# Hybrid decoder layer on one core: four heads of the samples' state products behind each piece of the gates' stage instead of sixteen behind each fourth

## What is computed

```python
# S_t = e^{g_t} S_{t-1} + beta_t k_t (v_t - e^{g_t} S_{t-1}^T k_t)^T ;  o_t = S_t^T q_t / sqrt(dk)
u_new = u_c - jnp.einsum('bhcd,bhde->bhce', w_c, S)
o = (jnp.einsum('bhcd,bhde->bhce', q_c * jnp.exp(G_c)[..., None], S)
     + jnp.einsum('bhcs,bhse->bhce', qk_c, u_new))
```

## Time and profile before

| | before |
|---|---|
| median of 3 runs | 2876.35 us (2874.61 to 2878.93) |
| the profiled execution's own time | 2873.98 us |
| its span, first to last instruction | 2872.4 us |
| mean granted TensorE clock | 0.957 |
| PE busy (matmul) | 2694.1 us, 94% of the span |
| DVE busy | 1658.9 us, 58% |
| ACT busy | 1344.4 us, 47% |
| POOL busy | 429.7 us, 15% |
| DMA | 505.31 MB, mean 176 GB/s |

### The profile page before, as it was taken

One profiled execution on the slowest core, in us unless ns is written; L12 is line 12 of the kernel. 1 busy time (PEld: TensorE's weight loads), 2 busy tenths in 40 slices (PEclk: granted clock), 3 DMA queues, 4 the chain that ended last, 5 costly groups with the idle time before them and its releaser, 6 DMA issues.

```text
span 2872.4 us, 57080 instructions
## 1 busy us (share of the span) xinstructions
PE 2694.1 (94%) x21133; PEld 2651.4 (92%) x21133; DVE 1658.9 (58%) x2851; ACT 1344.4 (47%) x2024; POOL 429.7 (15%) x813
## 2 busy tenths in 40 slices
PE   6989898888888989999999999899999999999997
PEld 4989898888888889999999999899999999999987
DVE  4747474747474656553335555555666656776664
ACT  4535353534344445443334434344555545665553
POOL 1324151515151505000000000000011000100000
PEclk9999999999999999999999999999999999999999
DMA  5545353535353535666665555755898566986552
GB/s 168 166 119 156 113 157 109 161 104 159 103 159 110 154 109 155 173 188 191 183 195 158 174 179 168 232 170 160 261 312 289 181 197 206 318 286 194 164 164 91
DMA packets 449338, 505.31 MB, mean 176 GB/s; under 512 B 27713, under 2 KB 429882, under 8 KB 446338
## 3 DMA queue, kind: packets, MB, share of 16 engines
q1 hardware_dynamic: 415264, 415.42, 48.1%
q0 software_dynamic: 24640, 86.42, 9.3%
q10 hardware_dynamic: 9282, 1.24, 0.3%
HBM read 477.10 MB, written 26.49 MB: 175 GB/s over the span
## 4 chain that ended last, share of the span: by engine, by line
PE 76%; POOL 8%; DMA 4%; issue 4%; DVE 3%; ACT 3%; POOLq 0%; ACTq 0%; DVEq 0%; SPq 0%
PE bank L668 75%; POOL prod L539 4%; POOL sol L542 4%; ACT whi L941 1%; DMA blk<-blk_scratch 1%; DMA raw<-in_w_ffn_down 1%; DMA raw<-in_w_o 1%; DMA sol_scratch<-sol 1%; DMA DT<-sol_scratch 1%; DVE wlo L1233 0%; ACT xhi L955 0%; DVE E L1285 0%; POOLq L73 0%; POOL sol_scratch L564 0%; POOL DT L568 0%
## 5 line engine op out<-in xcount | busy, mean ns | idle before, releaser
L668 PE MATMUL bank<-xhi,whi 128*128 128x264 f32 x5520 | 1618.9, 293 | 34.4 <-DVE wlo L1233 17.0
L668 PE MATMUL bank<-xlo,whi 128*128 128x264 f32 x5520 | 1593.3, 289 | 0.0
L668 PE MATMUL bank<-xhi,wlo 128*128 128x264 f32 x5520 | 1590.3, 288 | 0.0
L1233 DVE TENSOR_TENSOR wlo<-raw,whi 128x1024 fp32r<-128x1024 f32 x828 | 1012.1, 1230 | 817.6 <-ACT whi L941 815.4
L941 ACT ACTIVATE whi<-raw 128x1024 fp32r<-128x1024 f32 x828 | 872.3, 1058 | 926.3 <-PE bank L668 850.1
L668 PEld LDWEIGHTS bank<-xhi,whi 128*128 128x128 f32 x5520 | 1067.4, 193 | 40.9 <-issue 32.1
L668 PEld LDWEIGHTS bank<-xlo,whi 128*128 128x128 f32 x5520 | 1067.9, 193 | 2.6 <-issue 1.9
L668 PEld LDWEIGHTS bank<-xhi,wlo 128*128 128x128 f32 x5520 | 1064.4, 193 | 0.0
L668 PE MATMUL bank<-ahi,whi 128*128 128x264 f32 x704 | 200.6, 285 | 3.7 <-DVE wlo L1233 3.7
L668 PE MATMUL bank<-ahi,wlo 128*128 128x264 f32 x704 | 200.6, 285 | 0.0
L668 PE MATMUL bank<-alo,whi 128*128 128x264 f32 x704 | 200.2, 284 | 0.0
(11 more groups left out here) (279 smaller groups left out, 1902.5 us busy)
## 6 DMA issues: line engine op xcount, KB each, us to landing
raw<-in_w_in SPq DMA_DIRECT2D x356, 512.0 KB, 3.9
raw<-in_w_ffn_gate SPq DMA_DIRECT2D x88, 512.0 KB, 5.0
raw<-in_w_ffn_up SPq DMA_DIRECT2D x88, 512.0 KB, 4.7
raw<-in_w_ffn_down SPq DMA_DIRECT2D x96, 384.0 KB, 3.3
raw<-in_w_gdn_out SPq DMA_DIRECT2D x64, 512.0 KB, 3.6
chunkS<-in_state_gdn POOLq DMA_DIRECT2D x16, 1024.0 KB, 7.6
raw<-in_w_sconv_out SPq DMA_DIRECT2D x32, 512.0 KB, 3.6
raw<-in_w_o SPq DMA_DIRECT2D x32, 512.0 KB, 4.5
```

Source lines behind the costliest of these rows:

```text
L668: return pe.matmul(out, lhsT, rhs, start=start, stop=stop)
L1233: dve.tensor_tensor(wlo[:, at_ % SPLIT, :, :], raw[:, at_ % RAW, :, :], f32(whi[:, at_ % SPLIT, :, :]), ALU.subtract).then_inc(lo_ready, 1)
```

## The change

The sixteen products behind pieces 3 and 7 of an iteration become four behind each of its eight pieces. Heads, order and results are the same. PE's wait for a load of states moves from behind pieces 3 and 7 to behind pieces 0 and 4; `s_used` is still raised behind pieces 3 and 7.

```diff
-                elif ph.name == "gates" and j % 4 == 3:
-                    c = j // 4
-                    pe.wait_ge(s_in[c], 16 * (it + 1))
-                    for i in range(16):
+                elif ph.name == "gates":
+                    c, quarter = j // 4, j % 4
+                    if quarter == 0:
+                        pe.wait_ge(s_in[c], 16 * (it + 1))
+                    for i in range(4 * quarter, 4 * quarter + 4):
                         m = mm(bank[4][:, ds(it * 64 + 32 * c + 2 * i, 2)], chunkS[:, c, i, :],
                                kqs[:, 8 * c + i // 2, ds(it, 1), :].rearrange("p a b -> p (a b)"))
-                    m.then_inc(s_used, 1)
+                    if quarter == 3:
+                        m.then_inc(s_used, 1)
```

## The result

| | before | after |
|---|---|---|
| median | 2875.54 us (4 runs, 2874.61 to 2878.93) | 2859.13 us (4 runs, 2857.62 to 2859.96) |
| the profiled execution's own time | 2873.98 us | 2857.62 us |
| mean granted clock | 0.957 | 0.964 |

The ratio of after to before is 0.994, with a 95% interval of 0.9923 to 0.9957. The change takes 16.4 us off the median. The forecast was 2857.8 us, from 2852.0 to 2864.5.

What follows compares the result with a forecast made beforehand. PE was taken to bound the kernel, slowed by clock drops in the gates' stage. 21.65 - 0.45 - 2.70 - 0 = 18.5 us off 2873.98 gave 2855.5, plus 2.37 carried over 2857.8 us; range 2852 to 2864.5.

Steps and rivals of the forecast that it cites:

- Step 1: Gates' stage: low-clock stretches behind the batches of short passes all go once the batches are spread; gain 21.65 us.
- the likeness with the groups' stage: Groups' stage: eight float32 passes behind each piece, 3.81 us apart, keep clock 1.00; taken to hold for two-column passes.
- Rival 2: Gates' stage: the clock falls as often as before, nothing of the 21.65 us gained; 2879.5 us, chance 0.04.
- Step 2: Gates' stage: forty-eight more transitions between pieces and short passes cost 0.45 us, at most 4.3.
- Rival 1: Gates' stage: short two-column batches are dear, transitions cost 4.3 us instead of 0.45; 2861.7 us, chance 0.07.
- Step 3: End of the gates' stage: four products hide less of the wait for `xlo`, PE idles some 2.9 us; 2.70 us lost.
- Step 4: Behind the stage's last batch: the low stretch stays, 0 us; the other end is a gain of 1.54 us.
- rival 3: End of the gates' stage: no low stretch follows; 2856.3 us, chance 0.05.
- Step 5: States' transfers in the gates' stage: loads land in 14.1 us at worst against 18.1 allowed, never late; 0 us.
- Rival 4: Gates' stage: PE waits for states behind pieces 0 and 4, run slower; 2882 us or more, chance 0.02.

Runs made afterwards that it cites:

- e4: Kernel before, but each product of samples 0 to 5 has 128 moving columns instead of two; 2859.90 us, ratio 0.9943.
- e3: Kernel before with only PE's wait for the states' load moved to behind pieces 0 and 4, products left in place; 2872.90 us, ratio 0.9994.
- e5: Changed kernel with each group of four products made twice, so eight behind each piece; 2912.54 us, ratio to before 1.0141.
- e2: Changed kernel with four products behind the second and twelve behind the fourth piece, instead of four behind each; 2875.39 us, ratio to before 0.9999.
- e1: Changed kernel with eight products behind every second piece instead of four behind each; 2854.11 us, ratio to before 0.9928.
- e6: Changed kernel, but in the last iteration the sixteen products of heads 16 to 31 stand together behind the last piece; 2854.42 us, ratio to before 0.9931.
- e8: Changed kernel unaltered, measured again; 2857.18 us, ratio to before 0.995.
- e9: Changed kernel with eight products behind every second piece and the last sixteen together, 128 moving columns wide; 2851.33 us, ratio to before 0.9928.

## Why the prediction was right

**Step 1, the low stretches: right, and their cause is shown.** The forecast was that all 21.65 us of the stage go. The trace of after has PEclk 1.00 from 1273.04 to 1509.46. The forecast also argued that two moving columns instead of 128 don't spoil the likeness with the groups' stage. That was a choice, and part of it was luck: e4 shows that at sixteen products the columns make all the difference, so the likeness held because the groups are short. e3 excludes the moved wait, e5 the share, e2 the mere breaking up, and e4 shows that what the array moves in a batch decides. TensorE: Matmul & The Clock Gate in the Trainium skill (section on HAM oscillation) gives waits that idle the engine between bursts as the cause. At the end of the stage the trace agrees in part: behind 2.83 us of idle time, and the 0.95 us of short passes ahead of it, the clock is 0.90. But idle time isn't the whole of it, since in the kernel before PE had none in 16.75 us and the clock was 0.90. Rival 2, which took that rule literally, is dead.

**Step 2, the transitions: right, a little too small.** Pieces are 3.813 us apart, where the forecast rounded to 3.81: 0.043 us over four pieces instead of 0.03, so 0.64 instead of 0.45 us. It isn't a price for each transition, though: e1, with two transitions in four pieces, takes 15.21 us as the kernel before does with one. After, it is 3.83 us from a group to the next behind pieces 0, 2, 4 and 6 and 3.80 behind the others, where e1 has its groups too; why is open. Rival 1 (4.3 us) is dead.

**Step 3, the end of the stage: right.** 3.78 us behind the last piece instead of 3.77, 2.83 us of them idle (2.9 forecast). e6 gives the 2.7 us back when the twelve products are put back.

**Step 4, the low stretch behind the stage: right in the trace of after, but the term was too narrow.** It was to stay, at 1.54 us, or go (rival 3, which the trace of after excludes). In e8, the same kernel, it was 6.8 us long, and the bounds should have had that too. The price was mis-sized as well. From PE's first matmul of `yb0` to the 192nd behind it, it takes 25.07 us before and 25.04 after, 23.98 in e6 without a low stretch, and 26.16 in e8. So one low stretch costs 1.1 us here and not 1.54, and the long one 1.1 more, not 3.13 in all as behind the first batch. Part of what the full clock gives back is spent again on a wait: after piece 2 of `yb0` PE now waits for the samples' outputs, as in e6:

```profile
1522.09 0.44 PE L834 MATMUL bank<-ident,so 128*128 128x128 f32 x2 [0.26 <-DVE so L1586]
```

In the chain that ended last e6 has DVE without a break from `xlo` to `so`, where after has PE.

**Step 5, the transfers: right.** They are issued 0.87 us after a group's end and land 7.1 us after that in the median, 12.1 at worst: 13.0 us against 18.1 allowed. Rival 4 is dead.

**The sum.** The stage is 265.33 - 247.05 = 18.28 us shorter, 18.5 forecast; the rest is step 2's 0.2 us. The profiled execution is 16.36 us shorter: of the 18.28, 1.42 were lost ahead of the stage (it starts at 1270.02 instead of 1268.60) and 0.52 behind it. Nothing in the change touches what lies ahead. In the other traces the stage starts between 1266.38 (e3) and 1279.11 (e2), and what follows `yb0`'s start takes from 1335.35 (e9) to 1342.14 us (e4), so 2 us is within what executions differ by on their own. I had carried the 2.37 us between the profiled execution and the median of before over to after, where it was 1.5. That the median was met within 1.3 us is in part luck: the profiled execution was 2.1 us above its forecast of 2855.5, and the difference carried over was 0.9 too high.

## What to carry to other kernels

Read the granted clock beside the busy time: an engine that is 100% busy in every stretch can be slow in some, and the loss shows in the work behind its cause. Busy time doesn't tell. Trainium Kernel Development and Optimization in the Trainium skill (section Performance Expectations) prefers the busy share of the weight loads, beside the share of peak FLOPs, to that of the matmuls, but the weight loads don't show this loss either: PEld was 16.75 of 16.75 us busy at 0.90 and 15.21 of 15.21 at 1.00. In this kernel, many small products with hardly any moving columns did best strewn between the large ones in short groups (up to eight of 0.22 us, while twelve brought nothing), or made wider, where that cost no time. What such a batch hides at the end of a stage has to be priced as well, and was had back by leaving that one batch whole.

## What the runs showed of the hardware that was not expected

- A pass with 128 moving columns takes as long as one with two: twelve stretches of 15.21 us in e4, the very length of the undisturbed ones with two. Work that costs no time bought 1.54 us for each low stretch that it kept away.
- Twelve products in a row lost as much as sixteen (fourteen low stretches each), eight lost nothing in 31 batches inside the stage (e1). The batches that escape come at regular distances.
- The same kernel can have a low stretch of 3.4 or of 6.8 us at the same place (after and e8), and batches of the same length escape or don't.
